# Value products of two head pairs issued back to back in one PSUM bank

## The reference, cut to what matters

```python
def block(args):
    i, qn, qr = args
    s = jnp.einsum('bqhn,bkhn->bhqk', qn, k_nope) + jnp.einsum('bqhp,bkp->bhqk', qr, kr)
    s = s.astype(F32) * MLA_SCALE
    s = jnp.where(key_pos[None, :] <= q_pos[:, None], s, -jnp.inf)
    p = jax.nn.softmax(s, axis=-1).astype(v.dtype)
    return jnp.einsum('bhqk,bkhv->bqhv', p, v)
...
mla = mla_o.reshape(B, S, MLA_WIDTH) * jax.nn.silu(g_mla)
```

## Time and profile before

| what | us |
|---|---|
| median of three runs | 745.33 (743.96 to 746.56) |
| the profiled execution | 743.97 |
| its span in the trace | 742.1 |
| TensorE busy | 705.5 (95%) |
| VectorE busy | 355.3 (48%) |
| ScalarE busy | 327.3 (44%) |

### The profile page before, as it was taken

The page is one execution under the profiler, slowest core; times in us unless marked ns, Lnnn a source line. Parts: engine busy times, 40 slices in busy tenths (PEclk is TensorE's granted clock), DMA queues, the critical chain, the costliest instruction groups (busy, mean ns, idle before and its releaser), DMA issues.

```text
span 742.1 us, 16684 instructions
## 1 busy us (share of the span) xinstructions
PE 705.5 (95%) x7025; PEld 546.4 (74%) x7025; DVE 355.3 (48%) x782; ACT 327.3 (44%) x779; POOL 75.6 (10%) x113
## 2 busy tenths in 40 slices
PE   2799999999999999999999999999999999999995
PEld 1486878788789986777766666777677889678884
DVE  0454380030202025777675576667671111389977
ACT  1254651121212137667656566645675667602100
POOL 0000000000000010101111201132113443000000
PEclk9999999999999999999999999999999999999999
DMA  9995300303001011000010000202756774103332
GB/s 293 396 375 174 114 0 1 114 0 97 0 1 57 1 43 51 9 14 11 10 11 1 1 1 1 59 1 76 240 183 222 274 267 175 60 1 116 123 132 85
DMA packets 35301, 70.31 MB, mean 95 GB/s; under 512 B 6626, under 2 KB 17979, under 8 KB 33564
## 3 DMA queue, kind: packets, MB, share of 16 engines
q1 hardware_dynamic: 30602, 47.73, 19.8%
q0 software_dynamic: 4016, 20.97, 8.1%
q10 hardware_dynamic: 610, 0.55, 0.3%
HBM read 62.26 MB, written 6.07 MB: 92 GB/s over the span
## 4 chain that ended last, share of the span: by engine, by line
PE 90%; DVE 3%; SPq 2%; DMA 2%; ACT 1%; issue 1%; another core or an unknown queue 1%; DVEq 0%; ACTq 0%
PE banks L1988 21%; PE banks L2174 8%; PE banks L2000 6%; PE banks L2302 5%; PE banks L2383 4%; PE banks L2403 3%; PE banks L2152 3%; PE banks L2512 3%; PE banks L2514 3%; PE banks L2513 2%; PE banks L2090 2%; PE banks L2009 2%; PE banks L2452 2%; PE banks L2471 2%; PE banks L2495 2%; DMA s_x<-in_x_prompt 2%
## 5 line engine op out<-in xcount | busy, mean ns | idle before, releaser
L1044 ACT ACTIVATE s_z<-banks 128x512 f32<-128x512 f32 (+3 forms) x40 | 19.6, 501 | 130.0 <-PE banks L1988 130.0
L1988 PE MATMUL banks<-s_w_parts,s_h_b 128*128 128x272 f32 (+3 forms) x328 | 68.0, 323 | 0.0
L1253 ACT ACTIVATE s_z<-banks 128x512 f32<-128x512 f32 (+2 forms) x88 | 41.4, 517 | 47.1 <-PE banks L2383 46.3
L1417 DVE COPY s_zs<-banks 8x512 f32<-8x512 f32 (+3 forms) x6 | 3.5, 576 | 118.5 <-PE banks L1962 118.5
L1988 PEld LDWEIGHTS banks<-s_w_parts,s_h_b 128*128 128x128 f32 x328 | 49.3, 189 | 4.9 <-issue 1.7
L1244 ACT ACTIVATE s_z<-banks,s_temps 128x896 f32<-128x896 f32 (+7 forms) x64 | 47.2, 742 | 11.6 <-DVE s_temps L1712 8.6
L1988 PE MATMUL banks<-s_w_parts,s_h_a 128*128 128x256 f32 (+2 forms) x256 | 49.7, 314 | 0.0
L1988 PE MATMUL banks<-s_z_r,s_h_b 128*128 128x512 f32 (+1 forms) x152 | 48.8, 387 | 0.0
L2383 PEld LDWEIGHTS banks<-s_ident,s_z 128*128 128x128 f32 x288 | 33.3, 141 | 11.8 <-issue 5.5
L2383 PE MATMUL banks<-s_ident,s_z 128*128 128x128 f32 x288 | 39.8, 274 | 1.6 <-DVE s_z L1728 1.6
L1988 PE MATMUL banks<-s_z_r,s_h_a 128*128 128x512 f32 x128 | 40.9, 395 | 0.0
(11 more groups left out here) (391 smaller groups left out, 1520.7 us busy)
## 6 DMA issues: line engine op xcount, KB each, us to landing
s_z<-in_w_ada SPq DMA_DIRECT2D x16, 512.0 KB, 12.2
s_temps<-in_w_in SPq DMA_DIRECT2D x3, 2048.0 KB, 7.7
s_x<-in_x_prompt SPq DMA_DIRECT2D x8, 512.0 KB, 11.8
s_z<-in_w_ada SPq DMA_DIRECT2D x1, 4096.0 KB, 13.8
s_kt<-in_w_out SPq DMA_DIRECT2D x8, 512.0 KB
s_temps<-in_x_prompt SPq DMA_DIRECT2D x8, 512.0 KB
out_y_prompt<-s_temps SPq DMA_DIRECT2D x7, 512.0 KB
s_temps<-in_w_in SPq DMA_DIRECT2D x2, 832.0 KB, 14.2
```

Of the source, the lines that this page charges most:

```text
L1253: nc.scalar.activation(PTb[r % 3][:, 4 * g:4 * g + n, :], banks[:, 4 + (groups(r) + g) % 2, 0:P * n].rearrange("p (j q) -> p j q", j=n), A ...
L1988: last = nc.tensor.matmul(banks[:, proj_bank(c, t), 0:WIDTH[c]], h_[half][:, k, n0:n0 + P], w_, start=(k == 0 and n == 0), stop=(k == KT - ...
```

## The change

Where a small pair ends one step after a large pair, the small pair's products are issued right behind the large pair's, in step r + 2, into columns 128 to 255 of the same bank 6, without the wait on `mixed`. The two `mix` instructions are issued together at the large pair's step, r + 3, and the first of them waits for the products of both. The special place for the last small pair (step 48) goes.

```diff
+        def leads(p):
+            return (p + 1 < N_PAIRS_OF_HEADS and PAIRS[p][0] >= PAIRED and PAIRS[p + 1][0] < PAIRED and
+                    last_step(p + 1) == last_step(p) + 1)
+        def follows(p):
+            return p > 0 and leads(p - 1)
+        def pair_columns(p):
+            return slice(P, 2 * P) if follows(p) else slice(0, P)
         def mixed_at(p):
-            soon = PAIRS[p][0] < PAIRED or p == N_PAIRS_OF_HEADS - 3 or (p + 1 < N_PAIRS_OF_HEADS and last_step(p + 1) == last_step(p) + 1)
+            if follows(p):
+                return mixed_at(p - 1)
+            soon = PAIRS[p][0] < PAIRED or leads(p)
             return last_step(p) + (4 if soon else 5)
...
-                dve.wait_ge(pv_done, p + 1)
-                nc.vector.tensor_tensor(mixT[:, hp, P * i:P * i + P], banks[:, 6, 0:P], gT(i)[:, hp, :], ALU.mult).then_inc(mixed, 1)
+                dve.wait_ge(pv_done, p + 2 if leads(p) else p + 1)
+                nc.vector.tensor_tensor(mixT[:, hp, P * i:P * i + P], banks[:, 6, pair_columns(p)], gT(i)[:, hp, :], ALU.mult).then_inc(mixed, 1)
...
-                if p > 0:
+                if p > 0 and not follows(p):
                     pe.wait_ge(mixed, p)
...
-                            if s == len(STEPS):
-                                products(N_PAIRS_OF_HEADS - 2)
                             weights_turned(r)
-                            for p in range(N_PAIRS_OF_HEADS - 2):
-                                if last_step(p) == r - 1:
+                            for p in range(N_PAIRS_OF_HEADS - 1):
+                                if last_step(p) == r - 1 and not follows(p):
                                     products(p)
+                                    if leads(p):
+                                        products(p + 1)
```

More of the change, by code:

```diff
@@ L2301, in products @@
                         block = PTb[s % 3][:, par * (i + 1) + j, :] if i < PAIRED else PTb[(s - 1 + par) % 3][:, j, :]
-                        last = nc.tensor.matmul(banks[64 * par:64 * par + 64, 6, 0:P], V(j, 2 * hp + par), block,
+                        last = nc.tensor.matmul(banks[64 * par:64 * par + 64, 6, pair_columns(p)], V(j, 2 * hp + par), block,
                                                 start=(j == 0), stop=(j == i))
```

## The result

The changed kernel took 750.83 us (median of 4 executions), the kernel before 745.94 beside it: 1.0067 times as long, 95% interval 1.0043 to 1.0091. Forecast were 745.4 and no difference. Two further measurements of the same changed kernel, of 12 executions each, gave 1.0033 [1.0018, 1.0047] and 1.0020 [0.9995, 1.0044], the last of them not clear of 1. So it is slower, by less than the first result says, and the size moves from one measurement to the next. The question is in two parts: which waits are new, and what makes up the rest.

What follows compares the result with a forecast made beforehand. The prediction took TensorE's own issue time, busy 95% of the span, as the bound. Gains of 3.0 us against 3.05 given back summed to nothing from the median 745.33, with an uncertain extra 0.1: 745.4, range 743.0 to 747.6.

Steps and rivals of the forecast that it cites:

- Seam and gains: TensorE at the 14 joined pairs: the small pair's separate visit goes, 3.0 us gained; the seam between pairs costs nothing.
- C: Rival at the seams: each costs a visit's 0.15 anyway, 2.1 us in all, so 747.4; chance 0.07.
- B: Rival at the seams: products wait for ScalarE's copies, 0.5 at five to seven seams, 747.8 to 748.8; chance 0.09.
- D: Rival in the softmax stretch: pieces run on time set elsewhere, nothing changes; chance 0.67 together with the forecast.
- slow starts: TensorE's first work after products runs 0.10 longer; after a new stop 0.05, at five places, 0.25 given back.
- visits: TensorE going over to a group of half-width products and back: 0.34 us each where full-width work stands on both sides.
- Rival A: Turns need no cover from the small pair's products, so all 3.0 us comes: 742.3; chance 0.17.
- Given back: Turns losing cover wait for VectorE's scaling: waits 2.8 plus slow starts 0.25, 3.05 us in all.
- turn of 20: TensorE's turn in step 20, already waiting 1.44 for VectorE's chain: 0.40 us more wait.
- turn of 44: TensorE's turn in step 44, with no spare time behind its scaling: 0.78 us lost, all of it wait.
- A stretched scaling: VectorE's scaling of step 44 took 1.89 instead of 0.75 beside GpSimd's memsets; the same meeting expected again.
- From one trace to the time: Whole kernel: sum 0 +/- 0.5 against the profiled 743.97 or median 745.33, so 745.4 with the uncertain extra 0.1.

Runs made afterwards that it cites:

- after_third: The changed kernel unaltered, measured a third time against the kernel before: 744.82 us, 1.0020 [0.9995, 1.0044].
- late: Changed kernel's 14 joins, but both pairs' products issued in step r + 3 between scores and turn, mixes at r + 4: 741.37 us, 0.9985 of the kernel before.
- j0: Kernel before with only the three pairs of block 0 (r = 4, 7, 10) joined: 746.63 us, 1.0012 of the kernel before.
- j1: Kernel before with only the four pairs of block 1 (r = 36, 39, 42, 45) joined: 746.98 us, 1.0008 of the kernel before.
- before_head_split: Kernel before with sample pieces of steps 20 and 23 ahead of the turn and step 29's piece moved to 27: 746.07 us, 0.9983 of the kernel before.
- before_head: Kernel before, without joins, with the sample pieces of steps 20 and 23 moved ahead of the turn: 740.48 us, 0.9977 of the kernel before.
- late_head_split: Joins issued in step r + 3, pieces of steps 20 and 23 ahead of the turn, step 29's piece at 27: 743.81 us, 0.9973 of the kernel before.
- after_split: Changed kernel with one small sample piece (sixteen matmuls of 8 columns) moved from step 29 to 27: 750.51 us, 1.0049 of the kernel before.
- after_fill: Changed kernel with 17 unused transposes filling TensorE's stops around the turns of 19 and 20: 745.91 us, 1.0050 of the kernel before.
- after_head: Changed kernel with the sample pieces of steps 20 and 23 moved ahead of the turn: 742.50 us, 0.9991 of the kernel before.
- late_head: Joins issued in step r + 3, pieces of steps 20 and 23 ahead of the turn: 743.71 us, 0.9957 of the kernel before; again 739.51, 0.9962.

## Why the prediction was wrong, step by step

- **Seam and gains.** These held. The seam costs 0.01 and waits for nothing: rivals C and B are refuted, by the rows of 433 to 437 and the list of waits, and D by the turns' new waits. In the clean trace (after_third) all products together take 34.63 us from start to next start where they took 36.77, 2.14 less; the slow starts that went with the visits, eleven places, are 0.98. Gained: 3.1, forecast 3.0. The Trainium skill (TensorEngine Tiling (Array Packing), Tiling Modes, Key Properties) says that only a change of the mode drains the engine, not a change of the tile; this trace agrees, with 0.01 at a seam against 0.15 for the group's own entry and exit.
- **Rival A**, no cover needed, is refuted by six waits instead of two.
- **Given back.** I compare, place by place, the distance from one start to the next on TensorE in the trace of before and in the clean one. That holds more than the list of waits shows: an engine that stopped runs its first matmul longer, too. What grew:

| place | before | clean | extra | forecast |
|---|---|---|---|---|
| turn of 16 | 1.18 | 1.44 | 0.26 | 0.26 |
| turn of 19 | 1.08 | 1.62 | 0.54 | 0.42 |
| turn of 20 | 2.68 | 2.49 | -0.19 | 0.40 |
| turn of 22 | 1.29 | 1.62 | 0.33 | 0.20 |
| turns of 17, 26, 31 | | | 0.50 | 0.17 |
| turn of 32 | 1.48 | 1.71 | 0.23 | 0.58 |
| turn of 44 | 1.85 | 2.52 | 0.67 | 0.78 |
| slow starts | | | 0.33 | 0.25 |
| piece of step 11 | 0.89 | 1.30 | 0.41 | - |
| query's transposes, step 21 | 0.70 | 1.30 | 0.60 | - |
| query's projections, step 24 | 0.55 | 1.30 | 0.75 | - |
| query's transposes, step 33 | 0.66 | 1.03 | 0.37 | - |

  The places of the forecast cost 2.67 where I had 3.05: each within 0.35, but for the turn of 20, to which TensorE came 0.60 later. The first step that failed is that its list was of turns alone, each against VectorE's scaling. The last four places cost 2.13, and 3.1 - 2.67 - 2.13 is the 1.6 or 1.7 us that the clean trace lost. Three of the four wait for a copy by ScalarE and the one of step 33 for VectorE's work on a piece (line 1697). Two of them belong to the piece at the end of steps 20 and 23: it writes bank 7, ScalarE copies it behind the two exponentials of the step, and the query's work of the next step wants the bank. First ScalarE of the trace after (start, length, line), then of the trace of before, and TensorE's next row in before:

```profile
453.66 0.20 ACT L1257 ACTIVATION_READ_ACCUMULATOR s_z<-banks,s_temps 128x1 f32 x1
453.75 0.58 ACT L1222 ACTIVATE s_temps<-banks 64x512 f32<-64x512 f32 x1
```
```profile
451.00 0.58 ACT L1209 ACTIVATE s_temps<-banks 64x512 f32<-64x512 f32 x1
```
```profile
451.64 0.65 PE L2161 MATMUL banks<-s_ident,s_z 128*96 128x128 f32 x4
```

  Before, the copy ends at 451.58 and the transposes start at 451.64; after, 454.33 and 454.39. The distance is the same 0.06 that I had used for turns that wait. The wait was there before, so short (0.15 from the starts) that it has no row, and any time saved ahead of it comes back as more of it. The piece of step 11 is the same with another copy. ScalarE and TensorE, before and after:

```profile
414.13 0.59 ACT L1148 ACTIVATE s_qt<-banks 96x512 f32<-96x512 f32 x1
```
```profile
414.82 1.45 PE L2326 MATMUL banks<-s_w_uq,s_temps 128*32 128x384 f32 x4
```
```profile
416.08 0.59 ACT L1161 ACTIVATE s_qt<-banks 96x512 f32<-96x512 f32 x1
```
```profile
416.77 1.45 PE L2339 MATMUL banks<-s_w_uq,s_temps 128*32 128x384 f32 x4 [0.37 <-issue]
```

  0.10 behind the copy both times. With these four the forecast would have been 2.1 us slower, 747.5, and with the turn of 20 taken as it then comes, 0.60 later and so with 0.60 less to wait, 1.5 slower, 746.9. Both are inside the range given, on the side of slower, and well below the 750.83 measured: these places are what the forecast missed of the change, not all of what the first result has more.
- **A stretched scaling.** It met the memsets again, as forecast. VectorE, GpSimd and the turn of 44 in the trace after, against the earlier trace rows:

```profile
551.82 1.87 DVE L1741 TENSOR_SCALAR s_z<-s_z,s_temps 128x1024 f32<-128x1024 f32 x1
```
```profile
550.97 0.95 POOL L888 DMA_INDIRECT s_temps<-in_cache_k_rope,s_idx  x1 [0.30 <-issue]
551.90 1.23 POOL L944 MEMSET s_z<- 128x640 f32 x2
```
```profile
553.74 1.09 PE L2396 MATMUL banks<-s_ident,s_z 128*128 128x128 f32 x8 [0.63 <-DVE s_z L1741]
```

  The scaling started 0.08 ahead of the first memset and took 1.87 instead of 0.75; it ended 0.56 behind the second. The Trainium skill (SBUF — State Buffer, SBUF: two separate sides) has the first to start keep the shared port. Whether this trace agrees is open, and the prediction read it too simply: GpSimd was not idle when the scaling started, its gather of line 888 ran from 550.97 to 551.92, and starts on GpSimd are rough in these profiles. In late the first memset starts 0.45 ahead of the scaling, which then takes 1.33 and again ends 0.56 behind the second. What these traces show is that the scaling is done 0.56 us after the last memset.
- **From one trace to the time.** The prediction took the clock of 1.00 for a property of the kernel. It was one of the execution: a fall of 3.4 to 13.7 us at steps 26 to 31 stands in 16 of the 19 profiles beside that of before, j0, j1 and before_head_split among them, and is missing in before_head, late_head_split, after_third and before itself only. This is the second step that failed, a term that the sum did not have: time at the low clock, on which the next paragraph has the numbers.

**What stays open.** The change by itself is 1.6 us, 0.2%. The three measurements say 0.67, 0.33 and 0.20%. Time at the low level, worked out as 2 x (1 - granted clock) x span and averaged over all executions of a kernel, was 16.0 us for the changed kernel and 13.8 for before in the second measurement, 14.5 and 13.9 in the third. So the changed kernel has 0.6 to 2.2 us more of it, worth at most half that, which fits 0.3 and 0.2%. In the first it was 17.6 for the changed kernel; of before only the profiled execution's clock is on record, 0.995 or 7.4 us. If the other three had 13.8, before's mean was 12.2: 5.4 more, worth up to 2.7, and 4.3 with the 1.6, an estimate of 0.58%, inside the interval of the first result. So four executions of each, with one of before at an uncommonly high clock, can be the rest of it; that isn't shown. The average holds the start and the end of the kernel too, which the change doesn't touch, so it is a weak witness. That the joined order draws more or longer falls has more for it: the other kernels that join in step r + 2 have more than before beside them too (after_split 16.1 against 12.6, after_fill 15.5 against 12.0, after_head 14.9 against 13.8), and the four measurements of kernels that join in step r + 3 have not (12.7 against 13.8, 12.4 and 12.5 against 12.6, 12.2 against 13.9). Each of these differences has a standard error of 1 to 1.7, so no single one shows it, but all five point one way. How the joined order does it is not shown; what exactly calls the fall was not found, and both remedies tried for it failed.

## What to carry to other kernels

Before work that follows a group of matmuls is moved ahead of them, look for every later instruction whose start stands at the fixed hand-over distance (0.06 to 0.10 us here) behind another engine's end, through each engine and each buffer: such a pair has no slack, though the list of waits has no row for it, and gives back all that is saved ahead of it. Where cover is needed, moving both groups into the covered place (late_head, 0.4% faster than before in both of its measurements: 0.9957 [0.9935, 0.9978] and 0.9962 [0.9943, 0.9981]) does better than joining them at the earliest one (after_head, 0.9991 [0.9972, 1.0010]). Not all of the 0.4% is the join: the two moved pieces alone gave 0.9977 [0.9956, 0.9998] in another measurement (before_head), and in the traces without a fall the joins in step r + 3 add 0.4 to 0.6 us to their 1.35 (late_head_split against before_head). And for effects under 1% read several executions' clocks before a trace is taken as the kernel's own: here one pair of traces was 4.77 us apart where the change is worth 1.6.

## What the hardware showed that was not expected

- The granted clock of a TensorE that is 100% busy falls to 0.50 (1.2 GHz) for about 3.4, 6.8 or 10.2 us behind sixteen matmuls of 8 columns, in 16 of 20 profiles: 486.7 to 493.6 in one profile of the changed kernel, not at all in another. It moved with these matmuls when they were moved. With full-width transposes put between them the low stretch was 13.7, 6.8 and 10.2 us in three kernels.
- At full clock a round of one full-width transpose and two matmuls of 8 columns takes 0.58 us where the two alone take 0.23.
- A scaling on VectorE of 0.75 us takes 1.87 or 1.89 when GpSimd ends a gather and starts two memsets of 1.2 us together 0.08 to 0.12 after its start, and 1.33 when the first memset starts 0.45 ahead of it (late). Both times it ends about 0.56 us behind the last memset.
